# A one-core decoder step: biases as three bf16 parts, one gather tile for 32 tokens, and its output in four column groups

## What is computed

```
logits = (xf @ w_router) + b_router
vals, idx = lax.top_k(logits, TOP_K)
probs = jax.nn.softmax(vals, axis=-1)
combine = einsum('nk,nke->ne', probs, one_hot(idx, N_EXPERTS))
for e in range(N_EXPERTS):
    g = minimum(xf @ w_gate[e] + b_gate[e], SWIGLU_LIMIT)
    u = clip(xf @ w_up[e] + b_up[e], -SWIGLU_LIMIT, SWIGLU_LIMIT)
    hdn = (u + 1.0) * (g * sigmoid(SWIGLU_ALPHA * g))
    out = out + combine[:, e:e + 1] * (hdn @ w_down[e] + b_down[e])
```

## Time and profile before

| | us |
|---|---|
| median of three runs | 1340.11 |
| profiled execution, first to last instruction (span) | 1338.6 |
| TensorE busy | 1295.3 |
| VectorE busy | 508.0 |
| ScalarE busy | 179.5 |
| GpSimd busy | 79.1 |

### The profile page before, as it was taken

The page is one execution under the profiler, slowest core; times in us unless marked ns, Lnnn a source line. Parts: engine busy times, 40 slices in busy tenths (PEclk is TensorE's granted clock), DMA queues, the critical chain, the costliest instruction groups (busy, mean ns, idle before and its releaser), DMA issues.

```text
span 1338.6 us, 19293 instructions
## 1 busy us (share of the span) xinstructions
PE 1295.3 (97%) x7441; PEld 648.4 (48%) x7442; DVE 508.0 (38%) x981; ACT 179.5 (13%) x325; POOL 79.1 (6%) x107
## 2 busy tenths in 40 slices
PE   6999689999999999999999999999999999999996
PEld 4777467564544444444444444444444444443532
DVE  2899996542232232232323232222222232223232
ACT  3111126220100000101000000000000000010102
POOL 2532220120000000000000000000000000000000
PEclk9999889999999999999999999999999999999999
DMA  9934312468999999999898989898989898989671
GB/s 291 322 127 152 136 63 95 190 248 342 396 414 374 413 374 388 398 361 423 364 417 360 419 358 418 357 422 364 423 362 423 355 422 356 420 357 421 261 316 37
DMA packets 84376, 439.59 MB, mean 328 GB/s; under 512 B 7983, under 2 KB 30639, under 8 KB 35427
## 3 DMA queue, kind: packets, MB, share of 16 engines
q1 hardware_dynamic: 83219, 437.11, 81.4%
q0 software_dynamic: 976, 1.96, 0.5%
q10 hardware_dynamic: 144, 0.00, 0.0%
HBM read 437.46 MB, written 2.43 MB: 329 GB/s over the span
## 4 chain that ended last, share of the span: by engine, by line
PE 82%; DVE 8%; issue 6%; ACT 2%; DVEq 1%; DMA 0%; POOL 0%; SPq 0%; ACTq 0%; POOLq 0%
PE ps L1001 33%; PE ps L1060 16%; PE ps L979 11%; PE ps L1084 7%; PE ps L992 4%; DVE ws L1305 4%; PE ps L788 4%; PE ps L1053 3%; PE ps L910 2%; PE ps L805 1%; DVEq L1304 1%; DVE ws L1277 1%; PE ps L918 1%; PE ps L937 0%; DVE ws L1289 0%
## 5 line engine op out<-in xcount | busy, mean ns | idle before, releaser
L1001 PE MATMUL ps<-ring,ws 128*64 128x512 f32 x2032 | 451.5, 594 | 0.0
L1001 PEld LDWEIGHTS ps<-ring,ws 128*64 128x64 f32 x2032 | 141.5, 137 | 298.9 <-issue 298.9
L1060 PE MATMUL ps<-ring,ws 128*64 128x512 f32 x992 | 218.6, 592 | 0.0
L1476 DVE TENSOR_TENSOR acc<-ps,acc 128x1024 f32<-128x1024 f32 x48 | 58.8, 1224 | 285.9 <-PE ps L1084 285.9
L805 PE MATMUL ps<-ws,ring 128*128 128x288 f32 x640 | 159.7, 413 | 0.7 <-issue 0.7
L1456 DVE TENSOR_SCALAR ws<-ps 64x1024 f32<-64x1024 f32 x32 | 38.9, 1217 | 310.5 <-PE ps L1001 310.5
L979 PE MATMUL ps<-ws 128*128 128x64 bf16 x2304 | 145.3, 227 | 0.0
L979 PEld LDWEIGHTS ps<-ws 128*128 128x128 bf16 x2304 | 141.8, 170 | 2.9 <-issue 0.8
L805 PEld LDWEIGHTS ps<-ws,ring 128*128 128x128 f32 x640 | 123.8, 194 | 35.5 <-issue 0.8
L1060 PEld LDWEIGHTS ps<-ring,ws 128*64 128x64 f32 x992 | 71.3, 138 | 143.4 <-issue 143.2
L1305 DVE SCALAR_TENSOR_TENSOR ws<-ws,par x240 | 113.7, 549 | 0.0
(11 more groups left out here) (187 smaller groups left out, 611.2 us busy)
## 6 DMA issues: line engine op xcount, KB each, us to landing
ring<-in_w_gate SPq DMA_DIRECT2D x127, 1024.0 KB, 7.0
ring<-in_w_up SPq DMA_DIRECT2D x127, 1024.0 KB, 9.2
ring<-in_w_down SPq DMA_DIRECT2D x124, 1024.0 KB, 7.0
ring<-in_w_in SPq DMA_DIRECT2D x20, 1024.0 KB, 11.3
ring<-in_w_conf_pw SPq DMA_DIRECT2D x4, 1024.0 KB, 6.4
ring<-in_w_out SPq DMA_DIRECT2D x4, 1024.0 KB, 6.7
ws<-in_w_down SPq DMA_DIRECT2D x2, 1024.0 KB, 9.5
acc<-in_x_prompt SPq DMA_DIRECT2D x2, 512.0 KB, 4.2
```

What stands on the lines that cost most here:

```text
L1001: ins = nc.tensor.matmul(ps[m * CAP:(m + 1) * CAP, bk + h, :], x_e[:, b, 2 * q + t, :], w[:, m, t, h * 512:(h + 1) * 512], start=False, st ...
L1060: ins = nc.tensor.matmul(ps[h * CAP:(h + 1) * CAP, bk, :], hid_t[:, b, k, :], w[:, h * 512:(h + 1) * 512], start=False, stop=(k == NT - 1))
L1476: V.tensor_tensor(acc[:, i, :], ps[:, bk:bk + 2, :].rearrange("p h n -> p (h n)"), acc[:, i, :], ALU.add).then_inc(s_add, 1)
```

## The change

Three things change.

1. Biases. A new bf16 table `bias` holds, for gate, up and down apart, three parts of each bias in rows 0-31, 32-63 and 64-95 (rounded value, rounded remainder, what remains). `pick` has ones in the three rows of an expert (`bias_rows`), so that one bf16 matmul adds the three parts. The number of bias matmuls stays the same. The tables are made by POOL: three DMAs of 32 rows for a table, then casts and subtractions.
2. Gather. The 32 tokens of tile 2 are copied to partitions 32-63 and 64-95 of the tile, and their three parts are stacked in `h_rows`, one below another; `rank` is copied the same way. One matmul for tile 2 takes the place of three, 56 instead of 72 in all.
3. Output. The output of tile 2 is computed for its 32 rows alone, in four matmuls of 256 columns, each in its own group of 32 of the array's columns; DVE adds four pieces of 32x256.

On PE, the end of expert 2's turn (gather of expert 3, down of 1) and the gate/up of expert 3 with the outputs between its chunks (`ps` is PSUM, `ws` the workspace that holds the token parts, selections, picks and biases, `ring` the weight ring): before

The diff, without semaphore declarations and the same edits for `down`:

```diff
@@ -190,12 +191,16 @@
-        h_split = take(3 * TILES * D // 2).bitcast(BF16).rearrange("p (s i d) -> p s i d", s=3, i=TILES)
...
+        h_split = take(3 * 2 * D // 2).bitcast(BF16).rearrange("p (s i d) -> p s i d", s=3, i=2)
+        h_rows = take(D // 2).bitcast(BF16)
...
+        bias = take(3 * D // 2).bitcast(BF16).rearrange("p (m d) -> p m d", m=3)
+        raw_bias = [y_e, x_e_w, y_e]
...
@@ -441,8 +445,6 @@
                 sp.wait_ge(filled, JOB["out11"] + 1)
-                for m, name in enumerate(("b_gate", "b_up", "b_down")):
-                    sp.dma_start(bias[m * E:(m + 1) * E, :], A[name][0]).then_inc(s_bias, 16)
                 load_gu(1, 2)
@@ -500,6 +502,10 @@
+                pool.wait_ge(s_const, 5)
+                pool.tensor_tensor(cntf[:, 0:E], ident[:, 0:E], ident[:, E:2 * E], ALU.add).then_inc(s_seed, 1)
+                pool.wait_ge(s_seed, 3)
+                pool.tensor_tensor(bias_rows[:], cntf[:, 0:E], ident[:, 2 * E:3 * E], ALU.add).then_inc(s_const, 1)
@@ -564,17 +570,49 @@
-                for n, i in enumerate(TILE_ORDER):
-                    if n == 2:
-
-                        pool.wait_ge(filled, JOB["out11"] + 1)
-                        pool.wait_ge(s_rest, 4)
-                        pool.memset(bias[3 * E:, :], 0.0).then_inc(s_bz, 1)
-                        pool.wait_ge(s_bz, 1)
+                def load_bias(m):
+                    for r in range(3):
+                        pool.dma_start(raw_bias[m][r * E:(r + 1) * E, :],
+                                       A[("b_gate", "b_up", "b_down")[m]][0]).then_inc(s_bias[m], 16)
+
+                def split_bias(m):
+
+                    pool.wait_ge(s_bias[m], 48)
+                    for s in range(3):
+                        n = (3 - s) * E
+                        ins = pool.tensor_copy(bias[0:n, m, :], raw_bias[m][0:n, :])
+                        if s == 2:
+                            ins.then_inc(s_btab, 1)
+                            break
+                        ins.then_inc(s_part, 1)
+                        pool.wait_ge(s_part, 4 * m + 2 * s + 1)
+                        n -= E
+                        pool.tensor_tensor(raw_bias[m][0:n, :], raw_bias[m][0:n, :], bias[0:n, m, :],
+                                           ALU.subtract).then_inc(s_part, 1)
+                        pool.wait_ge(s_part, 4 * m + 2 * s + 2)
+
+                def rest(n, i):
                     pool.wait_ge(filled, JOB[f"ht{i}b"] + 1)
                     for s in range(2):
                         pool.wait_ge(s_split, 3 * n + s + 1)
-                        pool.tensor_tensor(h_tok[:, i, :], h_tok[:, i, :], h_split[:, s, i, :], ALU.subtract).then_inc(s_rest, 1)
+                        rows = P if i < 2 else (2 - s) * T_S
+                        part = h_split[:, s, i, :] if i < 2 else h_rows[0:rows, :]
+                        h = h_tok[0:rows, i, :]
+                        pool.tensor_tensor(h, h, part, ALU.subtract).then_inc(s_rest, 1)
+
+                pool.wait_ge(s_m, NT)
+                load_bias(0)
+                load_bias(1)
+                pool.memset(bias[3 * E:, :, :], 0.0)
+                pool.memset(h_rows[3 * T_S:, :], 0.0)
+                split_bias(0)
+                pool.wait_ge(s_btab, 1)
+                load_bias(2)
+                rest(0, TILE_ORDER[0])
+                split_bias(1)
+                rest(1, TILE_ORDER[1])
+                rest(2, TILE_ORDER[2])
+                split_bias(2)
@@ -973,12 +1014,12 @@
                     for t in range(NT):
-                        n = 0
+                        z = ps[:, BK_X, t * CAP:(t + 1) * CAP]
                         for s in range(3):
-                            for i in range(TILES):
-                                ins = nc.tensor.matmul(ps[:, BK_X, t * CAP:(t + 1) * CAP], h_split[:, s, i, t::NT],
-                                                       sel[:, b, i, :], start=(n == 0), stop=(n == 3 * TILES - 1))
-                                n += 1
+                            for i in range(2):
+                                nc.tensor.matmul(z, h_split[:, s, i, t::NT], sel[:, b, i, :],
+                                                 start=(s == 0 and i == 0), stop=False)
+                        ins = nc.tensor.matmul(z, h_rows[:, t::NT], sel[:, b, 2, :], start=False, stop=True)
@@ -989,8 +1030,8 @@
-                            nc.tensor.matmul(ps[m * CAP:(m + 1) * CAP, bk + h, :], pick[:, b, m, :],
-                                             bias[:, h * 512:(h + 1) * 512], start=True, stop=False)
+                            nc.tensor.matmul(ps[m * CAP:(m + 1) * CAP, bk + h, :], pick[:, b, 0, :],
+                                             bias[:, m, h * 512:(h + 1) * 512], start=True, stop=False)
@@ -1080,9 +1121,14 @@
-                    for h in range(2):
-                        ins = nc.tensor.matmul(ps[:, bk + h, :], sel_t[0:rows, i * P:(i + 1) * P],
-                                               y_e[0:rows, h * 512:(h + 1) * 512], start=True, stop=True)
+                    if i < 2 or rows < P:
...
+                    else:
+                        for c in range(4):
+                            ins = nc.tensor.matmul(ps[c * T_S:(c + 1) * T_S, bk, 0:256], sel_t[:, 2 * P:T],
+                                                   y_e[:, c * 256:(c + 1) * 256], start=True, stop=True)
@@ -1095,8 +1141,7 @@
                 pe.wait_ge(s_split, 3 * TILES)
-                pe.wait_ge(s_bz, 1)
-                pe.wait_ge(s_bias, 48)
+                pe.wait_ge(s_btab, 2)
                 gather(0, 0)
@@ -1370,7 +1416,12 @@
-                    V.tensor_scalar(h_tok[:, i, :], acc[:, i, :], inv, None, ALU.mult).then_inc(s_hn, 1)
+                    ins = V.tensor_scalar(h_tok[:, i, :], acc[:, i, :], inv, None, ALU.mult)
+                    if i == 2:
+                        link(ins)
+                        for r in range(1, 3):
+                            ins = V.tensor_copy(h_tok[r * T_S:(r + 1) * T_S, 2, :], h_tok[0:T_S, 2, :])
+                    ins.then_inc(s_hn, 1)
@@ -1413,17 +1464,16 @@
-                picks = ident[:, :].rearrange("p (m e) -> p m e", e=E)
+                for r in range(1, 3):
+                    ins = V.tensor_copy(rank[r * T_S:(r + 1) * T_S, 2, :], rank[0:T_S, 2, :])
+                link(ins)
...
-                    for m in range(2):
-                        ins = V.tensor_copy(pick[:, b, m, :], picks[:, m, bass.ds(e, 1)].to_broadcast([P, CAP]))
-                    ins.then_inc(s_pick, 1)
+                    V.tensor_copy(pick[:, b, 0, :], bias_rows[:, bass.ds(e, 1)].to_broadcast([P, CAP])).then_inc(s_pick, 1)
@@ -1469,16 +1519,22 @@
+                    if i < 2 or whole:
...
+                    else:
+                        for c in range(4):
+                            a = acc[0:T_S, 2, c * 256:(c + 1) * 256]
+                            ins = V.tensor_tensor(a, ps[c * T_S:(c + 1) * T_S, bk, 0:256], a, ALU.add)
```

More of the change, by code:

```diff
@@ L206, in build @@
         sel_t = take(T_PAD)
-        pick = take(2 * 3 * CAP).rearrange("p (b m s) -> p b m s", b=2, m=3)
+        pick = take(2 * 2 * CAP // 2).bitcast(BF16).rearrange("p (b m s) -> p b m s", b=2, m=2)
         spare_row = take(D)
-        at[0] = max(at[0], WS - D)
-        bias = take(D)
         early_down = [w_rg_w[:, 0:D], w_rg_w[:, D:2 * D], ws[:, SLOT + D:SLOT + 2 * D], spare_row]
@@ L224, in build @@
         s_rt = sem("router_and_g_ffn_loaded")
-        s_bias = sem("bias_loaded")
-        s_bz = sem("rows_without_bias_cleared")
+        s_bias = [sem(f"{n}_bias_loaded") for n in ("gate", "up", "down")]
+        s_part = sem("bias_parts_steps")
+        s_btab = sem("bias_tables_ready")
         s_gfin = sem("g_final_loaded")
@@ L696, in _ @@
                             act.wait_ge(s_rest, 2 * n + s)
-                        act.copy(h_split[:, s, i, :], h_tok[:, i, :]).then_inc(s_split, 1)
+                        rows = P if i < 2 else (3 - s) * T_S
+                        part = h_split[:, s, i, :] if i < 2 else h_rows[0:rows, :]
+                        act.copy(part, h_tok[0:rows, i, :]).then_inc(s_split, 1)
                 for n, i in enumerate(TILE_ORDER):
@@ L730, in _ @@
                 sigmoid(1)
+                act.wait_ge(s_btab, 3)
                 output(0, 0, d_chunk(0, 1))
@@ L1052, in down_bias @@
                     for h in range(2):
-                        nc.tensor.matmul(ps[h * CAP:(h + 1) * CAP, bk, :], pick[:, b, 2, :],
-                                         bias[:, h * 512:(h + 1) * 512], start=True, stop=False)
+                        nc.tensor.matmul(ps[h * CAP:(h + 1) * CAP, bk, :], pick[:, b, 1, :],
+                                         bias[:, 2, h * 512:(h + 1) * 512], start=True, stop=False)
                 def down_rows(b, k0, rows, bk=BK_D):
@@ L1082, in spread_tile @@
                             pe.wait_ge(s_add, TILES * g + i)
-                    for h in range(2):
```

(26 more changed lines are left out.)

11 lines of the change are left out of this document (7 added, 4 removed).

## The result

The changed kernel takes 1262.38 us (median of 4 runs, 1260.92 to 1264.79) where the kernel before takes 1340.38: a ratio of 0.942, 95% interval 0.940 to 0.943. The forecast was 1251, range 1237 to 1265. The direction, the new bound and the pace were as forecast; the time is 11 us longer, and nearly all of that arises at the start, before the transfers run back to back.

What follows compares the result with a forecast made beforehand. TensorE bound the old kernel, weight loads the new. The 169th pair lands at 1121.4; its 3.5 us chunk, 108.4 of TensorE work, 16.3 to the span's end and 1.5 around it give 1251 us, range 1237 to 1265.

Steps and rivals of the forecast that it cites:

- The new bound: Over the experts, weight loads at 59.9 us per two experts bind instead of TensorE, whose pace falls to 57.2.
- Rival A: TensorE stays the bound throughout the experts; 112.2 us saved less 4.0 of late start gives 1232 us; chance 0.10.
- TensorE's parts: Gather, biases and tile 2's output on TensorE save 7.1 us per two experts, from 64.28 to 57.2.
- C: Rival: bf16 bias matmuls cost what f32 ones did, TensorE sets the pace at 61 us, total 1292; chance 0.04.
- B: Rival: never-pausing transfers run slower, 414 GB/s or 5.07 us a pair, giving 1263 us; beyond that, chance 0.11.
- TensorE's waits: PE waits for gate/up chunks to land mid-experts, 15 to 25 us in sum, none at the start.
- D: Rival: waiting for chunks drops TensorE to its 1.2 GHz level, pace 85.8 us per two experts, total 1673; chance 0.02.
- SP's waits for slots shrink to a fraction: Sign on the weight-load queue: SP's waits for free ring slots, 462.7 us before, become a fraction.
- The start: Before the experts, POOL's bias preparation delays casts, squares and transposes; the first gather comes 4.0 us late, near 295.6.
- The first table is taken as landed by 253.9: At POOL's bias preparation, DMA issues and memsets from 246.8 end at 253.9, with the first bias table already landed.
- The third split comes after the last subtraction and has some 30 us before the first down bias: POOL's third bias-table split was given about 30 us before its result is needed; no cost was added for it.
- These 4.0 us come back at once: In experts 0 and 1, shorter gathers and gate/up biases save 4.5 us before the seventh ring pair is freed.

## Why the prediction was right, and where it was not

**The new bound: right, and shown.** Removing bytes brought 23 us, adding some 20 us of TensorE work cost 1 to 3, and adding some 47 in all (3.0 us for two experts) brought TensorE's pace back. Rival A also had its number right for its own condition: 1232 with a gather at 295.6 is 1241 with one at 304.46, which is what the run with fewer bytes measured.

**TensorE's parts: right.** 57.40 us against 57.2 for two experts. The bf16 bias pair takes 0.22 to 0.24 us, so C is out. The quads run side by side in the tile-2 output as they did in the mixer. The drain that the Trainium skill (TensorEngine Tiling (Array Packing), Key Properties) speaks of, if it is in the 0.57 us at all, is at most the 0.11 over the mixer's 0.46.

**Transfers, 59.9 us for two experts and 4.99 for a pair: right** (59.65 and 4.98). The end from the 169th pair on, forecast at 3.5 + 108.4 + 16.3 = 128.2 us, took 1260.2 - 1131.63 = 128.6. B did not come: 420 to 423 GB/s, and not 414. That the measured time lies within 1 us of B's number, 1263, is chance; the time was lost at the start.

**TensorE's waits: right,** 18.1 us (15 to 25), all in the middle. D did not come: 17 waits of at most 1.3 us left the granted clock at 1.00.

**"SP's waits for slots shrink to a fraction": wrong.** SP always waits for the next slot, whoever is slow; 799 us (462.7 and, for the down chunks, 336.7) became 696. What tells the two cases apart is the time from issue to landing, 6.9 against 21.1.

**The start: the step that failed.** The chain was the right one up to the transposes (POOL, ScalarE's casts, the squares), with a landing mis-sized, and behind them a wait was missing. "The first table is taken as landed by 253.9": POOL took it up at 258.46. Issues of the changed kernel from 244 to 285 show why:

```profile
ws<-in_w_up SPq DMA_DIRECT2D x1, 1024.0 KB, 20.0
...
ws<-in_b_gate POOLq DMA_DIRECT2D x3, 128.0 KB, 8.7
ws<-in_b_up POOLq DMA_DIRECT2D x3, 128.0 KB, 12.2
ws<-in_b_down POOLq DMA_DIRECT2D x3, 128.0 KB, 2.7
```

The same 128 KB took 2.7 us when the DMA engines were idle and 8.7 to 12.2 beside weight loads. Moving tile 2's subtractions alone did not win it back, so this term can be named, but its own price was not measured by itself. With it tile 1's square came at 288.14 where the forecast's chain (280.24 + 3.7) has 283.9: 4.2 us. POOL's casts, 1.03 us and not 1.2, gave a little back; TensorE's low clock made its rows, and not ScalarE's casts, the last link there, by 0.5 us.

The other 5.4 us of the 9.6 are VectorE beside POOL. "The third split comes after the last subtraction and has some 30 us before the first down bias" was true of who needs its result, and I asked nothing else of it. From rank to gather the changed kernel took 6.27 us, where before it is 291.56 - 290.30 = 1.26, and the forecast had added 0.35; that is 4.7 us, and 0.8 more in the cast of the mask ahead of them. Holding that split moved the gather by 5.7. The kernel before had shown such a wait: the mask step of its last tile, 0.18 us elsewhere, took 1.66 and ended 0.04 us behind POOL's subtraction.

```profile
287.44 2.12 POOL L577 TENSOR_TENSOR ws<-ws 128x1024 f32<-128x1024 f32 x1 [1.16 <-ACT ws L697]
...
287.94 1.66 DVE L1391 TENSOR_SCALAR mask<-lgr 128x32 f32<-128x32 f32 x1
```

The Trainium skill (SBUF — State Buffer, two separate sides) has the rule that I did not weigh: certain VectorE instructions and GpSimd's share one pair of SBUF ports as an exclusive lock, held for a whole instruction, and the other side waits. The ends 0.04 us apart in the rows above agree with it. That POOL's split is the cause is shown by the run that held it; that the lock is the way it acts rests on these ends alone.

**"These 4.0 us come back at once": right, a little less.** With the gather at 295.15 the 13th pair lands at 343.9, as in the kernel before with a gather at 291.56: 3.6 us returned. In the changed kernel 13.6 us of lateness became 10.3 at the 13th pair, 3.3 returned, where the forecast had 4.5. So the 11.1 us between 343 and 354.1 are 9.6 of a later gather, 1.2 of this term and 0.9 of a reading (the 13th pair of the kernel before landed at 343.9, not at 343), less the 0.5 (4.5 - 4.0) that the forecast had left aside. Behind it nothing is won back.

**The range: it held, in part by luck.** Its main case had the start 2 to 7 us late; the gather came 13.6 us late, and 10.3 were left at the 13th pair. 1262.38 lies inside 1237 to 1265 because the range had room for part of B.

## What to carry to other kernels

When a change takes work from the bound, name the next bound and its pace first: the parts are then worth only the distance to it, and the start, which little behind it can absorb any more, counts almost in full (here 10.3 us of 13.6). Work on GpSimd has two prices beside its own time, the queue behind it on engines that wait in order, and the small VectorE operations that run beside it; put it where nobody needs VectorE between SBUF tiles. A late link moved out of one engine's way often returns at the next tile, so look at the whole chain after each move.

## What was not expected of the hardware

VectorE operations of 0.18 us took up to 2.9 us beside GpSimd's casts (1.03 us) and subtractions (2.12 us), the longest of them beside one of each back to back. Not all did: MAX8 and MATCH_REPLACE8 (0.20 and 0.18) and the product that reads PSUM (0.64 a piece) kept their times. Small loads from GpSimd's queue took 8.7 to 12.2 us beside weight loads and 2.7 without them. Transfers kept 420 to 423 GB/s in 26 slices, 819 us, without a pause, above the 414 of the kernel before in 344 to 400.
